# A routed mixture-of-experts layer on one core: expert blocks of 168 slots instead of 192, padded slots left out of the gathers, slot entries loaded once and copied on chip

## What is computed

```python
def swiglu(x, w_gate, w_up, w_down):
    return (jax.nn.silu(x @ w_gate) * (x @ w_up)) @ w_down

def moe(x, lp):                       # x: (1104, 1024)
    scores = jax.nn.sigmoid(x @ lp['router_w'])
    _, idx = lax.top_k(scores + lp['router_bias'], 8)
    gate = jnp.take_along_axis(scores, idx, axis=-1)
    gate = gate / jnp.sum(gate, axis=-1, keepdims=True) * 2.5
    # every token through its 8 experts, weighted by gate and summed,
    # plus one shared expert for all tokens
    return routed + swiglu(x, lp['w_sh_gate'], lp['w_sh_up'], lp['w_sh_down'])
```

## Time and profile before

| what | value |
|---|---|
| median of three runs | 2792.64 us |
| the profiled execution: its own time | 2795.52 us |
| its span, first to last instruction | 2793.7 us |
| instructions | 36499 |
| mean granted TensorE clock | 0.950 |
| TensorE busy with matmuls | 2474.0 us, 89% |
| VectorE busy | 1362.5 us, 49% |
| ScalarE busy | 1044.8 us, 37% |
| GpSimd busy | 579.3 us, 21% |
| moved by DMA | 395.23 MB |

### The profile page before, as it was taken

How to read it: one execution, slowest core, us unless ns; L and a number is a source line. 1 busy time by engine, 2 the same in 40 slices (tenths; PEclk the granted TensorE clock), 3 DMA queues, 4 the chain that set the end, 5 groups by cost and what they waited for, 6 DMA issues and landing times. The chain is left out here.

```text
span 2793.7 us, 36499 instructions
## 1 busy us (share of the span) xinstructions
PE 2474.0 (89%) x13126; PEld 1851.2 (66%) x13126; DVE 1362.5 (49%) x2701; ACT 1044.8 (37%) x1662; POOL 579.3 (21%) x452
## 2 busy tenths in 40 slices
PE   8888888899966679999998669999999999999990
PEld 4455556564455646666454448999989999989990
DVE  0545544200066601011266137777777777777764
ACT  1145533200023100000021026666666766666652
POOL 0020022000000000000035103344433444344423
PEclk9989989999999889999999889999999999999995
DMA  3000043210010040100113069999999999999964
GB/s 131 0 12 1 1 154 151 87 38 0 0 41 0 0 170 23 45 23 23 51 31 112 15 233 271 287 282 285 287 285 285 298 287 287 273 292 281 284 176 155
DMA packets 113752, 395.23 MB, mean 141 GB/s; under 512 B 41590, under 2 KB 50886, under 8 KB 85254
## 3 DMA queue, kind: packets, MB, share of 16 engines
q1 hardware_dynamic: 78390, 269.63, 27.3%
q0 software_dynamic: 35296, 124.70, 18.1%
HBM read 325.74 MB, written 69.13 MB: 141 GB/s over the span
## 5 line engine op out<-in xcount | busy, mean ns | idle before, releaser
L1934 PE MATMUL banks<-split 128*128 128x384 f32 x1792 | 538.2, 363 | 0.0
L2048 DVE TENSOR_TENSOR split<-rest,split 128x2048 fp32r<-128x2048 f32 x192 | 438.8, 2286 | 108.2 <-ACT split L1992 91.4
L1932 PE MATMUL banks<-split 128*128 128x192 f32 x2048 | 482.7, 256 | 0.0
L1954 PE MATMUL banks<-split 128*128 128x512 f32 x1536 | 406.8, 407 | 17.3 <-ACT rest L2005 14.6
L1932 PEld LDWEIGHTS banks<-split 128*128 128x128 f32 x2048 | 389.1, 192 | 2.7
L1992 ACT CAST split<-rest 128x2048 fp32r<-128x2048 f32 x192 | 359.3, 1904 | 65.0 <-DMA rest<-in_w_exp_gate 60.1
L1393 PE MATMUL banks<-big 128*128 128x368 f32 x1152 | 358.9, 475 | 14.5 <-DMA big<-in_w_merge 14.5
L1934 PEld LDWEIGHTS banks<-split 128*128 128x128 f32 x1792 | 338.9, 189 | 0.0
L1882 POOL DMA_INDIRECT y_rows<-rest x128 | 266.7, 2083 | 336.5 <-ACT rest L2005 299.0
L1954 PEld LDWEIGHTS banks<-split 128*128 128x128 f32 x1536 | 276.5, 190 | 71.9 <-ACT rest L2005 17.5
L1393 PEld LDWEIGHTS banks<-big 128*128 128x128 f32 x1152 | 220.0, 191 | 153.1 <-issue 17.0
(11 more groups left out here) (327 smaller groups left out, 3088.0 us busy)
## 6 DMA issues: line engine op xcount, KB each, us to landing
rest<-in_w_exp_gate SPq DMA_DIRECT2D x64, 1024.0 KB, 9.1
rest<-in_w_exp_up SPq DMA_DIRECT2D x64, 1024.0 KB
rest<-in_w_exp_down SPq DMA_DIRECT2D x64, 1024.0 KB, 7.1
big<-in_w_merge SPq DMA_DIRECT2D x8, 1536.0 KB, 6.3
big<-in_w_cols SPq DMA_DIRECT2D x11, 512.0 KB, 3.8
x_rows<-big SPq DMA_DIRECT2D x9, 512.0 KB
y_rows<-big SPq DMA_DIRECT2D x9, 512.0 KB, 2.6
big<-in_x_cols SPq DMA_DIRECT2D x3, 1472.0 KB, 17.7
```

Of the source, the lines that this page charges most:

```text
L1932: ins = pe.matmul(PS[:, banks[f], 0:CAP], wr[:, s, j, LO, at:at + 128], x[:, k, 0:2], start=False, stop=False)
L1934: ins = pe.matmul(PS[:, banks[f], 0:2 * CAP], wr[:, s, j, HI, at:at + 128], x[:, k], start=False, stop=(k == KD - 1))
L1954: ins = pe.matmul(PS[:, DBANK[c]], hr[:, a, f, HALF * hf:HALF * hf + 128], wr[:, s, DOWN, b, at:at + 512], start=(f == 0 and j == 0), stop ...
L2048: dve.tensor_tensor(wr[:, s, j, LO], raw[:, s, j], wr[:, s, j, HI].bitcast(F32), ALU.subtract).then_inc(parted[j], 1)
```

## The change

1. CAP is 168 instead of 192, HALF 84 instead of 96. What depends on them: the moving columns of L1931, L1934 (336), L1932 (168) and L1916 (84), the shapes of the element-wise work, the rows of gathers and scatters, the limit from which an expert gets a second block, and one more comparison in the count of overflows.
2. The gathers get a bound: a token number over T - 1 is left out of the transfer. The rows T and up of `x1_dram` and the two DMAs that filled them are gone. GpSimd sets `xg` to zero once, ahead of the first gather.
3. SyncE loads the entries once, into `gi`. VectorE copies them into `si` (`keep_entries`, two small copies at the head of each block, behind waits for the gather's landing and for `si_free`). SyncE loads the next entries after that copy (`si_made`) and ahead of the weights. The scatter and ScalarE's first `part` wait for the copy.

```diff
-CAP = 192
+CAP = 168
...
-        sp.dma_start(S.x1_dram[T:T + 128], S.x1[:, 0]).then_inc(x1_out, 16)
-        sp.dma_start(S.x1_dram[T + 128:T + CAP], S.x1[0:CAP - 128, 1]).then_inc(x1_out, 16)
-        sp.wait_ge(x1_out, 16 * (NT + 2))
+        sp.wait_ge(x1_out, 16 * NT)
...
         with sp.Fori(0, last) as it:
-            first = [first_slot(2 * it + s) for s in range(4)]
+            first = [first_slot(2 * it + 2 + s) for s in range(2)]
             e = [expert(2 * it + 2 + s) for s in range(2)]
             for s in range(2):
                 n = 2 * it + s
-                sp.wait_ge(xg_in[s], 32 * (it + 1))
-                entries(gi, gi_in, s, first[2 + s])
+                sp.wait_ge(si_made[s], 2 * (it + 1))
+                entries(s, first[s])
                 for j in range(3):
                     sp.wait_ge(parted[j], n + 1)
                     weights(s, j, e[s])
-                sp.wait_ge(si_free[s], it + 1)
-                entries(si, si_in, s, first[s])
-        ends = [first_slot(2 * last + s) for s in range(2)]
-        for s in range(2):
-            sp.wait_ge(si_free[s], last + 1)
-            entries(si, si_in, s, ends[s])
...
                 pool.indirect_dma_start(out=xg[0:HALF, s, hf], out_offset=None, in_=S.x1_dram,
-                                        in_offset=bass.IndirectOffsetOnAxis(ap=gi[0:HALF, s, 2 * hf:2 * hf + 1].bitcast(I32), axis=0)
-                                        ).then_inc(xg_in[s], 16)
+                                        in_offset=bass.IndirectOffsetOnAxis(ap=gi[0:HALF, s, 2 * hf:2 * hf + 1].bitcast(I32), axis=0),
+                                        bounds_check=T - 1, oob_is_err=False).then_inc(xg_in[s], 16)
...
                 pool.wait_ge(y_out[0], 32 * (turn + 1))
                 pool.sem_inc(si_free[0], 1)
+            pool.wait_ge(si_made[s], 2 * (turn + 1))
             pool.wait_ge(part_copied, 4 * (2 * turn + s) + 8)
...
         for s in range(2):
             pool.sem_inc(si_free[s], 1)
+        pool.memset(xg.rearrange("p a b c -> p (a b c)")[0:HALF], 0.0).then_inc(xg_zero, 1)
+        pool.wait_ge(xg_zero, 1)
         gather(0, 0)
...
             if p == 0:
-                act.wait_ge(si_in[s], 16 * (turn_ + 1))
+                act.wait_ge(si_made[s], 2 * (turn_ + 1))
...
+        def keep_entries(s, turn_):
+            dve.wait_ge(xg_in[s], 32 * (turn_ + 1))
+            dve.wait_ge(si_free[s], turn_ + 1)
+            kept, loaded = (v[0:HALF, s].rearrange("p (h w) -> p h w", h=2) for v in (si, gi))
+            dve.tensor_copy(kept[:, :, 0].bitcast(I32), loaded[:, :, 0].bitcast(I32)).then_inc(si_made[s], 1)
+            dve.tensor_copy(kept[:, :, 1], loaded[:, :, 1]).then_inc(si_made[s], 1)
+
         def body(it, ends):
             for s in range(2):
                 n = 2 * it + s
                 nxt = (1, it) if s == 0 else (0, it + 1)
                 more = not (ends and s)
+                keep_entries(s, it)
                 part_weights(s, it, DOWN)
...
-        S.x1_dram = nc.dram_tensor("x1_rows", [T + CAP, DM], F32).ap()
+        S.x1_dram = nc.dram_tensor("x1_rows", [T, DM], F32).ap()
```

More of the change, by code:

```diff
@@ L1796, in stage_experts @@
     raw_in = [[sem(f"e_{n}{s}") for s in range(2)] for n in ("wg", "wu", "wd")]
-    gi_in, si_in, xg_in, y_out = ([sem(f"e_{n}{s}") for s in range(2)] for n in ("gi", "si", "xg", "yo"))
+    gi_in, xg_in, y_out = ([sem(f"e_{n}{s}") for s in range(2)] for n in ("gi", "xg", "yo"))
     rounded, parted = ([sem(f"e_{n}{j}") for j in range(3)] for n in ("hi", "lo"))
@@ L1802, in stage_experts @@
     part_full, part_copied, zeros = sem("e_pf"), sem("e_pc"), sem("e_zero")
-    si_free = [sem("e_sf0"), sem("e_sf1")]
-    passed = sem("e_passed")
+    si_free, si_made = [sem("e_sf0"), sem("e_sf1")], [sem("e_sm0"), sem("e_sm1")]
+    passed, xg_zero = sem("e_passed"), sem("e_xz")
     GBANK, UBANK, DBANK = (2, 3), (4, 5), (6, 7)
@@ L1828, in expert, with entries @@
             return sp.value_load(S.blocks_i[0:1, 0, bass.ds(n, 1)], min_val=0, max_val=EXPERTS - 1)
-        def entries(dst, sems, s, first):
-            sp.dma_start(dst[0:HALF, s].rearrange("p (h w) -> p h w", h=2).bitcast(I32),
-                         S.table[bass.ds(first, CAP)].rearrange("(h p) w -> p h w", p=HALF)).then_inc(sems[s], 16)
+        def entries(s, first):
+            sp.dma_start(gi[0:HALF, s].rearrange("p (h w) -> p h w", h=2).bitcast(I32),
+                         S.table[bass.ds(first, CAP)].rearrange("(h p) w -> p h w", p=HALF)).then_inc(gi_in[s], 16)
         def weights(s, j, e):
@@ L1839, in _ @@
         for s in range(2):
-            entries(gi, gi_in, s, first_slot(s))
+            entries(s, first_slot(s))
         for s in range(2):
```

## The result

The changed kernel takes 2958.9 us (median of 4 runs, 2952.82 to 2964.1) against 2791.56 us before (4 runs): a ratio of 1.061, 95% interval 1.058 to 1.064. It is 6% slower. The forecast was 2769 us, faster, with a range up to 2800.

The account below looks back on a forecast made before the run. TensorE (98.6% busy) was taken as the bound, DMA engines near it at 95%. Blocks of 15.40 + 0.25 = 15.65 us, with end blocks and once-only parts, save 23.6 us: 2771.9 profiled, 2769 median; range 2742 to 2800.

Parts of the forecast that it names:

- TensorE per block: Expert stage: 336-column products save 0.64 us, transposes 0.17, products of 168 columns nothing; 16.21 us a block becomes 15.40.
- The column rival: Low weights' products on TensorE do shrink with 168 columns: a block of 15.33 us, 2747 us; chance 0.10.
- The number of blocks: Expert stage: routing the reference's inputs gives 66 blocks instead of 64, one pair more.
- The bound: Gathers: padded rows are left out. Rival: they are still moved, 15.95 us a block, 2788 us; chance 0.05.
- The DMA engines on the mean: Expert stage: 14.2 of 15.4 us a block, 92% busy instead of 95, so they don't become the bound.
- VectorE, ScalarE: Per block: two new copies cost 0.35 us, smaller element-wise work saves about as much; at most 80% busy, covered by TensorE.
- the rival of VectorE's wait: VectorE waits 6.4 us at the block's head for a scatter's landing: 16.75 us a block, 2840 us; chance 0.08.
- The waits: Waits for `si` go; gathered rows are late 0.5 us in every second block, 0.25 a block, ends none and 0.7.
- The divisor rule: A DMA uses the largest number of engines up to 16 dividing its rows: 84 rows land no sooner than 96.
- SyncE's queue: Entries load moves ahead of the weights, GATE and UP go together: nothing, or 1 to 2 us a pair if gathers are held up.
- the chain rival: Scatter, landing, gather, landing stays 23.9 us and binds: a block of 16.1 us, 2798 us, no change; chance 0.17.

Follow-up runs that it names:

- the weights first: The changed kernel, but SyncE issues a block's three weight loads ahead of the entries load and its wait: 2841.5 us, ratio 1.018.
- only 168 slots: The kernel before with CAP 168 instead of 192 (66 blocks) and nothing else: 2815.3 us, ratio 1.009.
- only the bound: The kernel before, 192 slots, with only the bound on the gathers and the fill of `xg`: 2784.5 us, ratio 0.997.

## Why the prediction was wrong

- **TensorE per block: right.** 15.40 us was forecast, 15.35 measured. The products of 168 columns saved nothing. The loads in the changed kernel are 0.15 us apart across 336 columns and 0.11 across 168, as across 192:

```profile
2116.48 0.19 PEld L1927 LDWEIGHTS banks<-split 128*128 128x128 f32 x1
...
2116.63 0.19 PEld L1929 LDWEIGHTS banks<-split 128*128 128x128 f32 x1
...
2116.74 0.19 PEld L1927 LDWEIGHTS banks<-split 128*128 128x128 f32 x1
```

  The column rival falls. (Its time was 2749 by the prediction's own sum, not the 2747 that it gave.) The gap that the prediction quoted from the Trainium skill ("TensorE: Matmul & The Clock Gate", "Back-to-back issue gap"), which counts columns alone, doesn't hold for that step: 168 and 192 columns take the same 0.11 us, and what they share is the load of 128 columns.
- **The number of blocks: right.** 2112 products of L1927 (32 x 66) were executed.
- **The bound: right.** The GpSimd queue has 19,920 packets of 4 KB in the stage, 8,832 for the gathers and 66 x 168 for the scatters, so padded rows are left out.
- **The DMA engines on the mean: right.** 14.2 us of packets a block was forecast; a share of 0.76 of 18.72 us is 14.2.
- **VectorE, ScalarE: right.** The copies take 0.16 us each, and the rival of VectorE's wait (0.08) falls: 1.9 us in all. ScalarE's waits for entries are gone.
- **The waits: this is the step that failed.** It allowed 0.5 us of lateness a pair, ends 0 and 1.4. Measured: 4.7 us a pair over the 32 pairs (151.6 us in 31 waits). The mechanism was named, and it was a rival with a chance of 0.17: the path scatter, landing, gather, landing, 23.9 us with 22.5 left to it. Three sizes in it were off. First, the 82 rows fewer were to shorten the path by up to 1.4 us; they shortened it by nothing (23.9 before; 24.1 with 168 slots alone, 24.0 with the bound alone, 24.1 with both and the loads spread). The divisor rule stood in the text as a sentence beside the rival instead of deciding between 1.4 and 0. Second, SyncE's queue was put at nothing, or 1 to 2 us a pair at the far end; the three loads in a burst lengthened the path by 3.2 us (27.3 against 24.1). Third, what a wait does to the clock was left out: 4.43 us at 0.58 are 1.9 us lost in the pair that was read. The rival's own sum gives the measured time once these sizes are put in: 27.3 + (15.40 - 8.76) + 1.7 = 35.6 us, and 1.9 for the clock make 37.5, where 37.4 were measured.
- **The account.** A pair was forecast at 31.3 us and took 37.4. Of the 6.1 us, 4.2 are the longer wait (4.7 instead of 0.5), 2.0 what a block loses besides its wait, most of it by the lower clock, and -0.1 the shorter blocks. 32 pairs give 196 us. The profiled execution, 2963.86 us, lies 192 over its forecast of 2771.9, and the median, 2958.9, lies 190 over 2769.
- **The range.** It took the chain rival as the far end on the slow side. But it priced that rival at the path of before, 23.9 us, though the working had just moved 3 MB of weights onto the moment of the gather. A path with no slack has no upper end at its old length.

## What to carry to other kernels

A block time at which TensorE is always busy can hide a latency path that fits exactly; before making the blocks shorter, add up that path from issue to landing to issue and compare it with what the shorter block leaves. Moving a wait ahead of transfers in a queue moves their traffic too: look at what small, urgent transfer starts at that moment. The number of rows of an indirect transfer wasn't free to choose here: scatters of 92 rows landed far later than those of 96, and those of 84 no sooner.

## What the runs showed of the hardware that I had not expected

- 92 rows in place of 96 made the kernel 276 us slower, with four times the packets for each indirect DMA (383 against 111).
- The scatters of 92 rows were late and the gathers of 92 rows were not (9.6 us to the transposes).
- The same wait can cost a block its clock or not. In the run with the weights first, two blocks begin their transposes after 3.04 us of idle time each, at 2058.57 and 2157.24 us. In the next 4.43 us the clock was 1.00 in one, with 30 products, and 0.50 in the other, with 16 (columns of the earlier trace rows); the blocks took 18.60 and 21.14 us. What decides between the two isn't shown.

```profile
2058.57:2063.00 4.43, 4.43 (x30) 3.77 (x31) 3.42 (x4) 2.18 (x5) 0.65 (x1) 1.00 1.04 289
2157.24:2161.67 4.43, 4.43 (x16) 3.75 (x17) 3.05 (x3) 0.88 (x2) 0.66 (x1) 0.50 1.06 283
```

- Beside GpSimd's fill of 3.51 us, VectorE's four small first writes of the stage took 3.60 us, before 0.43. The fill goes with it in every run: the same four writes of 128x44 took 0.66 us in "only 168 slots", which has no fill, and those of 128x32 took 3.58 us in "only the bound", which has it (the second and third fence below). It cost nothing here, since GpSimd's first gather starts 4.5 us after the stage's first work, as before (4.4):

```profile
1640.60 3.51 POOL L1890 MEMSET rest<- 84x4096 f32 x1 [94.22 <-issue]
1640.62 3.60 DVE L2087 TENSOR_SCALAR split<-base 128x44 fp32r<-128x44 f32 x4 [4.12 <-PEq L2223]
1641.20 2.03 SPq L1829 DMA_DIRECT2D rest<-slot_table  x2
1643.28 0.37 SPq L1835 DMA_DIRECT2D rest<-in_w_exp_gate  x1
1645.15 1.06 POOL L1863 DMA_INDIRECT rest<-x_rows,rest  x1 [1.05 <-issue]
```

```profile
1637.86 0.66 DVE L2084 TENSOR_SCALAR split<-base 128x44 fp32r<-128x44 f32 x4 [4.10 <-PEq L2220]
```

```profile
1634.79 3.51 POOL L1897 MEMSET rest<- 96x4096 f32 x1 [92.71 <-issue]
1634.82 3.58 DVE L2086 TENSOR_SCALAR split<-base 128x32 fp32r<-128x32 f32 x4 [4.11 <-PEq L2222]
```
